# The first mixer of a two-block transformer kernel rebuilt: modulations by tiles of features, head sums with tokens on partitions

## The reference, cut to what matters

```python
mods = jnp.split(silu(c) @ w_ada[i] + b_ada[i], 6, axis=-1)     # sh1, sc1, g1, sh2, sc2, g2
u = x * (1.0 + sc1) + sh1
proj = u @ w_in                                                  # q, k, v, g, gk_lr
log_a = log_sigmoid(gk_lr @ w_gk2 + b_gk) / 16                   # cumsum in chunks of 64, exp: decays
o = intra-chunk attention + recurrent state                      # 4 heads, dk 128, dv 256
o = o * rsqrt(mean(o * o, -1) + 1e-6) * g_norm
y = (o * silu(g)) @ w_out
x = layer_norm(alpha * x + (1.0 + g1) * y, ln_g, ln_b)
```

## Time and profile before

| | |
|---|---|
| median of three runs | 1114.73 us |
| the profiled execution | 1115.32 us, of it the span 1113.6 us |
| PE busy | 1026.0 us (92%) |
| DVE busy | 815.3 us (73%) |
| ACT busy | 505.0 us (45%) |
| DMA | 227.93 MB, mean 205 GB/s |
| chain that ended last | PE 80%, DVE 10%, issue 4%, ACT 3%, DMA 3% |

### The profile page before, as it was taken

How to read it: one execution, slowest core, us unless ns; L and a number is a source line. 1 busy time by engine, 2 the same in 40 slices (tenths; PEclk the granted TensorE clock), 3 DMA queues, 4 the chain that set the end, 5 groups by cost and what they waited for, 6 DMA issues and landing times.

```text
span 1113.6 us, 16482 instructions
## 1 busy us (share of the span) xinstructions
PE 1026.0 (92%) x6752; PEld 922.2 (83%) x6752; DVE 815.3 (73%) x1087; ACT 505.0 (45%) x669; POOL 63.9 (6%) x138
## 2 busy tenths in 40 slices
PE   0779988999999899998999999799899989999995
PEld 0678967898989799887898998588788979999995
DVE  4669797977878877658877566867775757777775
ACT  0463524334343555724434333544355555555553
POOL 3001110000000021100100000100000000000000
PEclk9999988999999999998999999899899999999998
DMA  8858774886787475424865454263334345555551
GB/s 338 342 195 299 276 294 162 303 324 254 285 309 279 169 274 175 154 92 154 323 243 192 164 199 156 100 218 114 114 118 148 117 143 175 182 183 202 172 186 60
DMA packets 35050, 227.93 MB, mean 205 GB/s; under 512 B 4096, under 2 KB 4224, under 8 KB 10144
## 3 DMA queue, kind: packets, MB, share of 16 engines
q1 hardware_dynamic: 25232, 167.01, 42.6%
q0 software_dynamic: 9744, 59.87, 14.3%
HBM read 225.82 MB, written 1.05 MB: 204 GB/s over the span
## 4 chain that ended last, share of the span: by engine, by line
PE 80%; DVE 10%; issue 4%; ACT 3%; DMA 3%; POOL 1%; DVEq 0%; POOLq 0%; ACTq 0%
PE ps L417 73%; DMA ada_raw<-ada 2%; DVE weight_lo L1414 2%; ACT weight_hi L1018 1%; DVE ada_acc L1456 1%; PE ps L618 1%; DMA weight_raw<-weights 1%; PE ps L628 1%; PE ps L524 1%; DVE dev L1571 1%; DVE dev L1565 1%; PE ps L799 1%; PE ps L789 1%; DVE att_s L1870 1%; PE ps L788 0%
## 5 line engine op out<-in xcount | busy, mean ns | idle before, releaser
L1414 DVE TENSOR_TENSOR weight_lo<-weight_raw,weight_hi 128x2048 fp32r<-128x2048 f32 (+1 forms) x188 | 361.5, 1926 | 112.9 <-ACT weight_hi L1018 112.7
L417 PE MATMUL ps<-act_hi,weight_hi 128*128 128x256 f32 x1400 | 353.0, 290 | 11.8 <-ACT gla_q L1022 5.6
L1018 ACT ACTIVATE weight_hi<-weight_raw 128x2048 fp32r<-128x2048 f32 (+2 forms) x168 | 299.9, 1786 | 128.2 <-PE ps L417 96.4
L417 PE MATMUL ps<-act_lo,weight_hi 128*128 128x256 f32 x1400 | 348.1, 287 | 0.0
L417 PEld LDWEIGHTS ps<-act_hi,weight_hi 128*128 128x128 f32 x1400 | 273.4, 195 | 23.1 <-issue 13.3
L417 PEld LDWEIGHTS ps<-act_lo,weight_hi 128*128 128x128 f32 x1400 | 273.7, 196 | 3.4 <-issue 1.0
L417 PE MATMUL ps<-act_hi,weight_lo 128*128 128x256 f32 x1400 | 186.9, 283 | 0.0
L417 PEld LDWEIGHTS ps<-act_hi,weight_lo 128*128 128x128 f32 x1400 | 175.5, 191 | 0.2
L417 PE MATMUL ps<-weight_hi,mlp_lo 128*128 128x512 f32 x256 | 101.8, 398 | 0.0
L417 PE MATMUL ps<-weight_hi,mlp_hi 128*128 128x512 f32 x256 | 101.6, 397 | 0.0
L1456 DVE SCALAR_TENSOR_TENSOR ada_acc<-ada_raw,c_act,ada_acc 128x2048 f32<-128x2048 f32 x35 | 82.2, 2349 | 9.7 <-DMA ada_raw<-ada 8.3
(11 more groups left out here) (312 smaller groups left out, 1270.8 us busy)
## 6 DMA issues: line engine op xcount, KB each, us to landing
weight_raw<-weights SPq DMA_DIRECT2D x144, 1024.0 KB, 5.0
ada_raw<-ada POOLq DMA_DIRECT2D x48, 1024.0 KB, 6.8
weight_raw<-weights SPq DMA_DIRECT2D x23, 512.0 KB, 3.6
row_g<-ln_rows POOLq DMA_DIRECT2D x4, 512.0 KB, 4.3
row_b<-ln_rows POOLq DMA_DIRECT2D x4, 512.0 KB, 5.0
att_bias<-rel_bias POOLq DMA_DIRECT2D x16, 128.0 KB, 3.4
square<-ada_rows POOLq DMA_DIRECT2D x3, 512.0 KB, 4.0
dev<-x_in SPq DMA_DIRECT2D x1, 1024.0 KB, 10.1
```

Of the source, the lines that this page charges most:

```text
L417: return e.matmul(o, a, b, start=start, stop=False, skip_group_check=True)
L1018: e.activation(weight_hi[h][:, 0:size], weight_raw[r][:, 0:size], ACT.Copy).then_inc(hi_full[h], 1)
L1414: ins = e.tensor_tensor(weight_lo[h][:, c], weight_raw[r][:, c], weight_hi[h][:, c].bitcast(F32), ALU.subtract)
```

## The change

- **Stage one.** Group 0 of `w_ada` is laid out so that a chunk holds all 1024 rows of one tile of 128 features (shift and scale). For each of eight tiles DVE sums the first three of the eight row blocks (one 128x256 TENSOR_SCALAR, two SCALAR_TENSOR_TENSOR), PE the other five, as ten fp32 matmuls of one column with `ada_raw` as the stationary operand, and two more for DVE's part (`first_mods`). A tile's input is made while the next chunk is fetched, and PE takes `gk`, `q0` and `q1` up tile by tile. `x_in` is fetched at once, the first weights at `ada_used` 1, 3, 5. Twelve matmuls on constants stand ahead.
- **Gates' chain.** ACT first evacuates `q0` and `q1`, splits chunk 4, and puts `split_hi(5)`, `k0` and `split_hi(6)` between the log and the exps. g moves ahead of v on PE (g0, g1, v0, v1, g2, g3, v2, v3), and g is token-major.
- **Heads.** Outputs have tokens on partitions, so ACT's Square sums them (`accum_out`), POOL makes the root, and DVE applies root and gate in one step; PE transposes the result (`gla_turn`) and ACT applies `g_norm`. Gone are L635, L642, L1537, L1543, L1741. The pieces of `w_out` go to banks 0 and 1 for tokens 0 to 127 and stand between the last heads' steps.
- **Modulations.** `mods_of` multiplies by one column of ones instead of 128. Group 2 is cut in halves of columns: the four half chunks for `sc0` stand in the mixer, the other four, and the gate row `rb`, in the first MLP, which now holds 4 half and 16 whole chunks (16 whole before, of groups 3 and 4).

```diff
-            e.wait_ge(ada_used, 3)
             e.dma_start(dev[:, :, :], x_in).then_inc(x_arrived, 16)
             e.dma_start(g_w2[:, :], w_gk2).then_inc(w2_in, 16)
             for j, size in enumerate(SIZES):
                 if j < N_RAW:
-                    e.wait_ge(ada_used, 5 + j)
+                    e.wait_ge(ada_used, (1, 3, 5)[j])
...
+            def first_mods(f):
+
+                slot = f % N_ADA_RING
+                raw = ada_raw[slot][:, :].rearrange("p (k n) -> p k n", k=KT)
+                e.wait_ge(ada_full[slot], 16 * (f // N_ADA_RING + 1))
+                if f >= 2:
+                    e.wait_ge(u_mods, f - 1)
+                for x in range(2):
+                    o, c = ps[:, 6 + f % 2, x:x + 1], slice(x * P, (x + 1) * P)
+                    for k in range(U_ROWS, KT):
+                        mm(o, raw[:, k, c], c_act[:, k:k + 1], start=(x == 0 and k == U_ROWS))
+                e.wait_ge(ada_used, f + 1)
+                for x in range(2):
+                    last = mm(ps[:, 6 + f % 2, x:x + 1], ada_acc[:, (2 * f + x) * P:(2 * f + x + 1) * P], ones_sq[:, 0:1])
+                last.then_inc(u_summed, 1)
...
+            for _ in range(U_BUSY):
+                e.matmul(ps[:, 5, 0:P], ones_sq[:, :], ident[:, :], start=True, stop=True, skip_group_check=True)
+            e.wait_ge(c_done, 1)
+            first = ((0, work_tiles(W["gk"], 1), P, 3), (1, work_tiles(W["q0"]), 256, 5),
+                     (2, [(q1_ps[:, n, :], 4) for n in range(2)], 256, 7))
+            for f in range(KT):
+                first_mods(f)
+                for j, outs, wide, begin in first:
+                    if f >= begin:
+                        first_chunk(j, outs, wide, range(f) if f == begin else (f - 1,))
+            for j, outs, wide, _ in first:
+                first_chunk(j, outs, wide, (KT - 1,)).then_inc(chunk_done, 1)
...
-            project(2, W["q1"])
...
+            v_half(5, 0, W["g0"])
+            v_half(5, 1, W["g1"])
+            gla_scores(0)
+            v_half(7, 0, W["v0"])
+            gla_scores(1)
+            v_half(7, 1, W["v1"])
+            gla_states(0)
+            v_half(9, 0, W["g2"])
+            gla_scores(2)
+            gla_out(0)
+            gla_scores(3)
+            gla_states(1)
+            v_half(9, 1, W["g3"])
+            gla_out(1)
+            v_half(11, 0, W["v2"])
+            gla_turn(0)
+            v_half(11, 1, W["v3"])
+            gla_turn(1)
+            gla_states(2)
+            e.wait_ge(*emptied(W["o0"]))
+            e.wait_ge(*emptied(W["o1"]))
+            out0_half(0, 0)
+            gla_out(2)
+            gla_states(3)
+            e.wait_ge(ket_out, GLA_H)
+            out0_half(0, 1).then_inc(chunk_done, 1)
+            gla_out(3)
+            out0_half(1, 0)
+            gla_turn(2)
+            for n in range(2):
+                mod_row(f"ra{n}", 1, n * HALF, ra_ps[n])
+            e.wait_ge(gated, 2 * GLA_H)
+            mods_of("sh0", 1, 8, 8, sh0_ps)
+            out0_half(1, 1).then_inc(chunk_done, 1)
+            gla_turn(3)
+            def last_mods():
+                e.wait_ge(mods_in, 1)
+                mods_of("sc0", 2, 0, 8, sc0_ps)
+            tail(0, [((lo_in, LO_GLA + 2 * h + 2), gla_hi, gla_lo, 2 * h) for h in (2, 3)], 2, last_mods)
+            e.wait_ge(mods_in, 2)
+            e.wait_ge(lo_in, LO_GLA + KT)
+            e.wait_ge(ra_in, 2)
...
+                e.wait_ge(u_mods, k + 1)
                 e.activation(act_hi[:, k, :], dev[:, k, :], ACT.Identity, bias=bias, scale=scale).then_inc(hi_in, 1)
-                if k % 2:
+                e.activation(square[:, k, :], dev[:, k, :], ACT.Identity, bias=bias, scale=scale).then_inc(hi_in, 1)
...
+                if k in (1, 3, 5):
+                    split_hi(k // 2)
...
             split_hi(3)
             evacuate(1, W["q0"], g_q[:, 0:2, :], halves(W["q0"]), GLA_DK ** -0.5)
+            e.wait_ge(chunk_done, 3)
+            e.activation(g_q[:, 2:4, :], q1_ps, ACT.Copy, scale=GLA_DK ** -0.5).then_inc(q1_in, 1)
+            split_hi(4)
             e.wait_ge(gate_read, GLA_H)
             n = own.of(e.activation(g_e[:, :], g_la[:, :], ACT.Abs))
             e.wait_ge(act_step, n)
             n = own.of(e.activation(g_e[:, :], g_e[:, :], ACT.Exp, scale=-1.0))
             e.wait_ge(act_step, n)
             e.activation(g_e[:, :], g_e[:, :], ACT.Ln, bias=1.0).then_inc(log_gate, 1)
+            split_hi(5)
+            evacuate(3, W["k0"], g_k[:, 0:2, :], halves(W["k0"]))
+            split_hi(6)
...
+                    if f:
+                        mods_of_tile(f - 1)
+                    e.wait_ge(ada_full[slot], 16 * (f // N_ADA_RING + 1))
+                    n = own.of(e.tensor_scalar(to, raw[:, 0, :], c_act[:, 0:1], None, ALU.mult))
+                    for k in range(1, U_ROWS):
+                        e.wait_ge(dve_step, n)
+                        ins = e.scalar_tensor_tensor(out=to, in0=raw[:, k, :], scalar=c_act[:, k:k + 1], in1=to,
+                                                     op0=ALU.mult, op1=ALU.add)
+                        if k < U_ROWS - 1:
+                            n = own.of(ins)
+                    ins.then_inc(ada_used, 1)
+                    if f:
+                        residue(f - 1)
+                    if f in (2, 4, 6):
+                        split_lo(f // 2 - 1)
+                mods_of_tile(KT - 1)
+                residue(KT - 1)
...
+                    e.scalar_tensor_tensor(out=dev_rows[:, t, vs], in0=gla_o_ps[:, t, :], scalar=head_root[:, h, t:t + 1],
+                                           in1=g_sg[:, t, vs], op0=ALU.mult, op1=ALU.mult).then_inc(gated, 1)
...
+            gla_states(2)
+            gated_head(2)
+            split_lo(15)
+            gla_states(3)
+            ada_halves()
+            gated_head(3)
+            out_residue(2)
+            ada_halves()
...
                 gate_half(f"ra{n}", 0, n)
-            for _ in range(3):
-                ada_chunk()
-            for i in range(3):
-                split_lo(J_OUT0 + 2 + i)
-                if i == 0:
-                    mods_of("sc0", 0, 4, 8)
-            ln_scales(0, 0, 4, 3, "sc0")
+            mods_first("sh0", 3, sh0_ps)
+            out_residue(3)
+            for _ in range(2):
+                ada_halves()
+            split_lo(J_OUT0 + 3)
+            mods_first("sc0", 4, sc0_ps)
+            ln_scales(0, 0, 4, 3, (mods_in, 2))
+            split_lo(J_OUT0 + 4)
...
+                    if m == 0 and i < 4:
+                        ada_halves()
+                    elif m == 0:
                         ada_chunk()
-                    split_lo(up_chunk(m, i) + 3)
-                    if fill and (i == n_blocks - 2 or i % 2):
-                        ada_chunk()
-                        if i < n_blocks - 2:
+                        if i % 2 == 0 and i < n_blocks - 2:
                             ada_chunk()
...
+            def head_power(h):
+
+                e.wait_ge(o_squared, 2 * h + 2)
+                n = own.of(e.tensor_tensor(head_sum[:, h, :], head_sum[:, h, :], rms_eps[:, :], ALU.add))
+                e.wait_ge(pool_step, n)
+                e.tensor_tensor(head_root[:, h, :], head_sum[:, h, :], minus_half[:, :], ALU.pow).then_inc(root_pow, 1)
```

More of the change, by code:

```diff
@@ new lines, in first_chunk @@
+            def first_chunk(j, outs, wide, tiles):
+                at = products(j, outs, act_hi, act_lo, KT, wide, True, False)
+                e.wait_ge(hi_full[j], 1)
+                e.wait_ge(lo_full[j], 1)
+                for k in tiles:
+                    e.wait_ge(lo_in, LO_U + k + 1)
+                    for n in range(len(outs)):
+                        o, one, two, three, start = at(n, k)
+                        mm(o, *one, start=start)
+                        mm(o, *two)
+                        last = mm(o, *three)
+                return last
@@ L629, in mod_row @@
                          skip_group_check=True).then_inc(mods_summed, 1)
-            def root_sum(k, n, tile, r):
-                for t in range(ST):
-                    if k == t == 0:
-                        e.wait_ge(root_mean, r)
-                    last = e.matmul(ps[:, 7, t * P:(t + 1) * P], tile[:, t * P:(t + 1) * P], ones_sq[:, :],
-                                    start=(k == 0 and t == 0), stop=(k == n - 1), skip_group_check=True)
-                if k == n - 1:
-                    last.then_inc(summed, 1)
@@ L640, in spread @@
[L640 to L649 removed]
+            e.wait_ge(consts_in, 5)
@@ new lines, in gla_out, with gla_turn @@
+                for t in range(ST):
+                    mm(gla_o_ps[:, t, :], a_of[h][:, t, :], g_v[:, t, vs], start=(t == 0))
+                e.wait_ge(states, 2 * (h + 1))
+                for c in range(1, NCH):
+                    p0 = CHUNK * (c % 2)
+                    last = mm(gla_o_ps[p0:p0 + CHUNK, c // 2, :], g_q[:, h, c * CHUNK:(c + 1) * CHUNK], g_st[:, c - 1, :])
```

(61 more changed lines are left out.)

497 lines of the change are left out of this document (188 added, 309 removed).

## The result

| | before | after |
|---|---|---|
| median of nine runs each, on the same chip | 1116.28 us (1111.89 to 1120.55) | 1122.6 us (1119.94 to 1126.51) |
| ratio, with its 95% interval | | 1.0069 (1.0049 to 1.0088) |
| profiled execution, of it the span | 1115.32, 1113.6 us | 1119.94, 1118.2 us |

What follows compares the result with a forecast made beforehand. It took DVE and the gates' chain of waits to bound the first 204 us, PE the MLP after. Terms of -6.6, -15.7, +8.7 and +1 made -12.6 us, 1115.3 to 1102.7, so 1102 us; range 1091 to 1119.

Steps and rivals of the forecast that it cites:

- part 1: Stage one until k0: one-column records at 0.115 us, k0 starts at 52 instead of 58.56 us, -6.6 us.
- Part 4: After 204 us: the MLP's four half chunks cost 1 us, one column in later sums 0.
- Rival B: Stage one: pauses at tiles keep PE's clock at half, kernel slower, 1124 us with six slow tiles; chance 0.18.
- wait for `weight_lo` 6: Mixer, at g0: PE ready at 68.8 us, the split done at 70.8, a wait of 2.0 us.
- waits for masks and states: Mixer: PE's scores wait 0.8 us for masks, heads 2 and 3's outputs 2.0 us for their states.
- wait of `sc0`: End of the mixer: PE ready at 153.4 us, DVE's half chunks and row gates until 157.3, 3.9 us.
- Rival A: Mixer and MLP: DVE's load and order give most of the gain back, 1108 to 1116 us; chance 0.18.
- the sum's 8.7: k0 to the end of `w_out`: new waits of PE where DVE is late, together +8.7 us.
- Rival C: Stage one: a one-column record costs only 0.056 us, k0 at 44 to 45 us, 1091 to 1096 us; chance 0.12.

Runs made afterwards that it cites:

- E1: The changed kernel with only stage one's sums multiplied by 128 equal columns instead of one; 1110.16 us, ratio 0.9949 to the kernel before.
- E3: The changed kernel with stage one's and the later sums all in 128 columns, no one-column matmul left; 1103.16 us, ratio 0.9893 to the kernel before.
- E2: The changed kernel with only the later sums in 128 columns, stage one left at one; 1116.33 us, ratio 0.9999 to the kernel before.
- E4: The kernel before with only its sums in `mods_of` multiplied by one column instead of 128; 1121.02 us, ratio 1.0043.
- E7: E3 with one half chunk moved ahead of head 2's gate; 1101.53 us, ratio 0.9878 to the kernel before.
- E11: E7 with the last half chunk moved ahead of head 3's residue too; 1098.38 us, ratio 0.984 to the kernel before.
- E12: E11 with DVE's split of chunk 6 moved ahead of the decayed q; 1094.46 us, ratio 0.9803 to the kernel before.

## Why the prediction was wrong, and where it was right

**The step that failed** is in part 1: "From there PE is the bound: five tiles 14.0 us". The price, 0.115 us, was right for a one-column record at full clock (0.114 at tile 0, 0.107 at tile 6). The clock was taken for granted as long as PE is busy. The runs show 0.207 to 0.213 us for tiles 2 to 5 without any idle time: the five tiles took 21.3 us for the 14.0, and the products among the tiles 20.1 for 14.4. Together that is k0's 12.8 us, within 0.2. E1 and E3 bring 0.112 us back with the columns alone. The row of 64 columns was read for its price and could not show this: it stands between wider matmuls, and is over after 1.4 us. Tile 3 did start where it was forecast, 21.49 us for 21.5, but by luck: there was no wait for its fetch, because half clock at tiles 1 and 2 had used up the time.

In the profiled execution the forecast was 1102.7 us and the time 1119.94, 17.2 us more: 12.8 until k0, 2.3 from k0 to the end of `w_out`, 2.7 behind the start of the MLP, and 0.6 less in the layer norm between.

**Part 4's "One column instead of 128 in later sums: 0"** failed for the same reason. The sums cost nothing more themselves; the products behind them did. The ratio falls from 1.0069 to 0.9999 with E2 and from 0.9949 to 0.9893 between E1 and E3, and E4's stands 0.0043 above the kernel before: 5 to 8 us of 1115.

**Rival B** had the right mechanism for stage one, with a chance of 0.18: half clock, the gain gone at three to four tiles, six tiles 1124 us. It named the single column as the case that no row shows, but its reason was pauses, and E3 shows that these matter little: they are in E3, and it is fast. That its 1124 us lies 1.4 us from the measured time is in part luck: six tiles at half would have put k0 at 73.6 us, it started at 64.8, and some 6 us of the loss come from the later sums, which B did not have. My argument against B, that from tile 5 on the runs of products leave PE no pause, looked at the wrong thing: the tiles ahead of the runs have no pause either, and tile 7, behind a run, fell too. The Trainium skill (TensorE: Matmul & The Clock Gate, HAM oscillation) describes bursts of matmuls between waits for DMA. E3's tile 3 agrees with it in a small way: after 2.92 us of waiting its 20 records take 4.12 us instead of 2.40. The changed kernel's tiles 2 to 5 are at half clock with no wait at all, so waits do not explain them.

**With the columns wide, the sum holds term by term.** E3 is at 1103.16 us for the forecast's 1102:

| | forecast | E3 | changed kernel |
|---|---|---|---|
| tile 3 waited for until | 21.5 us | 20.72 | no wait |
| k0 starts | 52 | 54.08 | 64.78 |
| wait for `weight_lo` 6 | 2.0 | 2.59 | 2.59 |
| waits for masks and states | 2.8 | 1.20 | 1.21 |
| wait of `sc0` | 3.9 | 4.42 | 4.42 |
| k0 to the end of `w_out` | 115.7 | 115.0 | 118.0 |
| MLP starts | near 175 | 175.91 | 189.33 |

k0 is 2.1 us late in E3 because tile 3 starts at half clock (1.7 us) and tile 5 waits 1.59 us for DVE's part, a wait that part 1 did not have; tile 3 came 0.8 us earlier than forecast. The waits for masks did not come. The gates' chain is covered as forecast: no idle PE between k0 and the wait for `weight_lo` 6. **Rival A** did not come: DVE is busy 97 of 118 us between k0 and the end of `w_out` in the changed kernel, 82%, and PE waits 8.2 us for it, for the sum's 8.7. E7, E11 and E12 show that 7 of these were DVE's order and not its load. **Rival C** is refuted: a one-column record costs what a 64-column one costs. (Its 423 GB/s stands in no row, whose highest rate is 292.) The MLP with its four half chunks takes about 1 us longer, as taken (178.5 us from its start to the product behind `m3`, 177.5 before), with DVE busy 138.84 of 158 us for the 138 forecast.

What stays open: what it is about narrow matmuls that lets the clock fall. The runs varied only the columns, and all these records come one per 0.11 us at full clock. Columns between 64 and 128 were not tried, and the later sums were run with one and 128 columns only.
